# A two-block network in one kernel: its first norms, first products and the loads ahead of them, rearranged into one stage

## The chip, the cores and the metric

The kernel runs on one core of a Trainium2 chip. The metric is the device time of one execution in microseconds (us), here the median of several executions. TensorE is called PE in the profile, its weight loads PEld, VectorE DVE, ScalarE ACT, GpSimd POOL, and SyncE, which issues most loads, SP.

## The reference

A sequence of 1024 tokens of width 1024 passes through two blocks; a context of 256 tokens takes part in the first one. Only the beginning matters here:

```python
mod   = split(silu(c)     @ w_ada + b_ada, 6)      # sh1, sc1, g1, sh2, sc2, g2
mod_c = split(silu(c_ctx) @ w_ada + b_ada, 6)      # sh1c, sc1c, ...
h_lat = rmsnorm(x,   norm1_g) * (1 + sc1)  + sh1   # 1024 tokens
h_ctx = rmsnorm(ctx, norm1_g) * (1 + sc1c) + sh1c  # 256 tokens
u, v, q, k, vv, r, af, ab, ga, gb = split(h_lat @ w_in, ...)
# the same for h_ctx; then gated linear attention over both, a chunk MLP,
# a merge, a SwiGLU; then a second block (RG-LRU, window attention, SwiGLU)
```

`rmsnorm` divides by the root of the mean square over the 1024 channels and multiplies by the norm's weight. Everything is float32. A product with a weight matrix is computed from high and low parts: weights and activations are each split into a rounded high part and the rest, and three matmuls (high by high, low by high, high by low) are summed in PSUM.

## The kernel before, in words

Activations lie transposed, channels in the 128 partitions (8 tiles of 128 channels), tokens along the free dimension. The tokens are worked in three parts: the context (256 columns, tiles `CH`, `CL`) and two halves of x (512 columns each, tiles `XH`, `XL`). Weights come in tiles of 128 output channels, 128x1024 elements or 512 KB, in one fixed order (`weight_order`): first `al` (the low-rank gate inputs), then `k` 0 to 3, `vv` 0 to 7, `q`, and so on through the program. Each is loaded by SP into one of two raw slots `WS`, rounded by ACT into one of four slots `WH` (line 242) and subtracted by DVE into `WL` (line 250). `weights_sp`, `weights_act` and `weights_dve` bring this up to a given tile; they stand in the program order of the engine that runs them. Every engine executes its instructions in that order, and `wait_ge` stops it until a semaphore has its value.

`stage0` does the first norm. PE computes the modulation rows from `w_ada`, 8 tiles of 128x2048 elements (1 MB each, `ada_pe`, line 570): 8 by 4 products of 512 columns, each of two matmuls. ACT squares x and the context (lines 501, 505), DVE adds the squares over the 8 tiles (line 513), PE sums them over the partitions (`columns_pe`, line 578), ACT takes the root (line 606), DVE the reciprocal and a diagonal matrix of it, and PE spreads that over all partitions (`spread_pe`, line 564). ACT copies the modulation rows out of PSUM (line 618), PE turns them into columns (line 596), and DVE makes the four small vectors of scales and shifts (lines 644 to 648). Then `modulated_dve` and `modulated_act` make the modulated input of a part, per channel tile: DVE scales (line 538), ACT adds the shift and rounds (line 521), DVE takes the rest (line 531). `stage0` does so for the context and for the first half of x; SP's loads in it stand in the order of lines 481 to 492.

`stage1` begins with `firsts`, three groups of four products (`al`, `k0`, `k1`, `k2`), one group for each part of the tokens: 96 matmuls of 256 columns for the context, and twice 96 of 512 columns. `products_pe` (lines 273 to 296) runs a group with the channel tile k outermost, so each k needs only the tile k of the activations. The low-rank output goes to `AL` (lines 777 and 855), the three others through the four `TMP` slots to memory (lines 395 and 432). At the start of `stage1`, SP, ACT and DVE each wait for all that `stage0` has ended (`gone`):

```python
def sp_():
    for t in gone:
        SPW.wait_ge(*t)
    sp.dma_start(WA0[:], D["walpha"]).then_inc(*wal_in.up())
    sp.dma_start(cmask[:], D["cmask"]).then_inc(*cm_in.up())
    sp.dma_start(cb[:], D["crow"]).then_inc(*cb_in.up())
    weights_sp(NW + NS)
```

ACT then applies silu to `cb` and copies `WAL` ahead of its first copy out of PSUM, and the second half of x is modulated between the groups of the context and of the first half (`second_act`, `second_dve`). After `firsts`, `stage1` runs its fill, the products of `k3`, `vv` and `q`, beside the gates' decays; later stages follow in the same manner.

Of the kernel before, what the change touches and what calls it, by code (L numbers as in the profile page):

```python
# [7 lines left out]
F = mybir.dt.float32  # L8
R = mybir.dt.float32r
# [9 lines left out]
NW = 4  # L19
# [104 lines left out]
def program(nc, D, out):  # L124
# [69 lines left out]
    w_in = [sig("in", f"weight_in{s}") for s in range(NS)]  # L194
    w_hi, w_lo = sig("ac", "weight_high"), sig("dv", "weight_low")
# [37 lines left out]

    def weights_act(upto):
        while made["hi"] < min(upto, len(order)):
            i = made["hi"]
            made["hi"] += 1
            ACW.wait_ge(*w_in[i % NS].at(i // NS + 1))
            if i >= NW:
                ACW.wait_ge(*used[i - NW])  # L240
            n = cols_of[i]
            ac.activation(WH[:, i % NW, 0:n], WS[:, i % NS, 0:n], ACT.Copy).then_inc(*w_hi.up())  # L242

    def weights_dve(upto):
        while made["lo"] < min(upto, len(order)):
# [4 lines left out]
            dv.tensor_tensor(WL[:, i % NW, 0:n], WS[:, i % NS, 0:n], WH[:, i % NW, 0:n].bitcast(F), ALU.subtract).then_inc(*w_lo.up())  # L250

    def weights_sp(upto):
        while made["in"] < min(upto, len(order)):
            i = made["in"]
            made["in"] += 1
            if i >= NS:
                SPW.wait_ge(*w_lo.at(i - NS + 1))
            if i in raw_used:
                SPW.wait_ge(*raw_used[i])
            sp.dma_start(WS[:, i % NS, 0:cols_of[i]], tiles[i]).then_inc(*w_in[i % NS].up())  # L260
# [181 lines left out]
    def stage0():  # L442

        CH, CL = CTX
# [4 lines left out]
        DIA = {"c": RB[:, 512:768], 0: RB[:, 512:1024], 1: RB[:, 0:512]}  # L449
        cc_in, xc_in = sig("in", "cc"), sig("in", "xc")  # L450
        x_in = [sig("in", f"x{k}") for k in range(8)]
        ad_in = [sig("in", f"ad{k}") for k in range(8)]
        silu = sig("ac", "silu_c")
        ada = sig("pe", "ada")
        squares, added = sig("ac", "squares"), sig("dv", "squares_added")
        colsum, rooted, recip = sig("pe", "column_sums"), sig("ac", "rooted"), sig("dv", "reciprocal")
        diag, spread = sig("dv", "diagonal"), sig("pe", "spread")
        mcopy, mturn, mods = sig("ac", "mods_copied"), sig("pe", "mods_turned"), sig("dv", "mods")
        shifted = sig("dv", "shifted")
# [4 lines left out]

        sums = [("c", k) for k in range(8)] + [(h, k) for k in range(8) for h in range(2)]
        total = {"c": RB[:, 0:TC], 0: ACC[:, 0:512], 1: ACC[:, 512:1024]}
        first_of = {"c": 0, 0: 8, 1: 9}
        slots = [k for k in range(24) if sums[k][1] > 0]
# [3 lines left out]

        def source(what, k):
            s, c = dst[what][0], dst[what][1]
            return s[:, k, c:c + size[what]]

        def added_of(what):
            last = max(j for j in range(24) if sums[j][0] == what)
            return added.at(slots.index(last) + 1)

        def sp_():
            sp.dma_start(VEC[:], D["vec"]).then_inc(*vec_in.up())
            sp.dma_start(ident[:], D["ident"]).then_inc(*ident_in.up())
            sp.dma_start(sc2[:], D["cc"]).then_inc(*cc_in.up())
            loads = {2: (0, 1), 3: (2, 3), 4: (4, 5), 5: (6, 7)}
            for k in range(8):
                sp.dma_start(AD[:, k, :], D["ada"][k]).then_inc(*ad_in[k].up())
                if k == 2:
                    sp.dma_start(XC[:], D["ctxT"]).then_inc(*xc_in.up())
                for x in loads.get(k, ()):  # L490
                    sp.dma_start(RES[:, x, :], D["xT"][x]).then_inc(*x_in[x].up())
            weights_sp(NW)

        def squares_act(j):
            what, k = sums[j]
            if what == "c":
                ACW.wait_ge(*xc_in.at(1))
            else:
                ACW.wait_ge(*x_in[k].at(1))
            if k == 0:  # L500
# [22 lines left out]
        def modulated_dve(what):  # L523
# [11 lines left out]
            for k in range(8):  # L535
# [3 lines left out]
                if k:  # L539
                    low(k - 1)  # L540
# [3014 lines left out]
```

## Time and profile before

| | |
|---|---|
| median of 3 runs | 3434.43 us (3432.78 to 3436.52) |
| profiled execution | 3435.87 us |
| its span | 3434.6 us |
| PE busy | 3270.4 us (95%) |
| DVE, ACT, POOL busy | 1929.5, 1373.2, 384.1 us |
| mean granted PE clock | 0.98 |

The span runs from the first to the last recorded instruction; all positions below are us from its start. The granted clock is 1.00 where PE gets its full 2.4 GHz and 0.50 where it gets 1.2 GHz. A row of a timeline gives the start, the duration, engine, line, operation, the tiles written and read, the count of merged instructions, and in brackets how long the engine had been idle and what ended that.

### The profile page before, as it was taken

What the parts mean: (1) busy time and instruction counts of PE and PEld (TensorE: products, weight loads), DVE (VectorE), ACT (ScalarE), POOL (GpSimd) and SP (SyncE); (2) the same over time, 40 slices, a digit from 0 to 9 for tenths busy, and PEclk for the clock granted to TensorE, in tenths of its full rate; (3) what the DMA queues carried; (4) which work ended last, traced back from release to release, by engine and by line L of the source; (5) the groups of instructions that cost most, each with busy time, mean ns of one, the idle gap of its engine ahead of it and who ended that gap; (6) DMA issues with size and microseconds to landing.
All of it is one profiled execution on the core that took longest, in us unless ns stands there. A gap on an engine that the chain in (4) does not pass through costs nothing. (4 is left out here: it accounts for less than half of the span.)

```text
span 3434.6 us, 39599 instructions
## 1 busy us (share of the span) xinstructions
PE 3270.4 (95%) x14862; PEld 2659.9 (77%) x14862; DVE 1929.5 (56%) x3098; ACT 1373.2 (40%) x2320; POOL 384.1 (11%) x605
## 2 busy tenths in 40 slices
PE   6999999989999999999999999999788899999998
PEld 3888888877788878888888888877555678888886
DVE  4474343454334387777545555655576487777443
ACT  4592232224333244333233356554576343333221
POOL 0121000001100200000010101111211100001011
PEclk8999999999999999999999999999899899999999
DMA  5365433344553423333763433444844523334752
GB/s 218 107 218 183 142 126 123 123 156 157 200 161 117 138 71 117 109 115 118 248 203 97 154 119 137 136 157 150 171 96 104 184 92 117 105 116 165 248 179 77
DMA packets 228045, 494.14 MB, mean 144 GB/s; under 512 B 21520, under 2 KB 84624, under 8 KB 226320
## 3 DMA queue, kind: packets, MB, share of 16 engines
q1 hardware_dynamic: 147728, 302.30, 27.7%
q0 software_dynamic: 80128, 189.30, 16.9%
q8 instruction: 120, 1.97, 0.2%
q14 instruction: 69, 0.57, 0.0%
HBM read 353.63 MB, written 137.89 MB: 143 GB/s over the span
## 5 line engine op out<-in xcount | busy, mean ns | idle before, releaser
L290 PE MATMUL p<-s_xh,s_wh 128*128 128x512 f32 x2256 | 905.6, 401 | 36.9 <-DVE s_tmp L401 12.3
L291 PE MATMUL p<-s_xl,s_wh 128*128 128x512 f32 x2256 | 888.7, 394 | 0.0
L292 PE MATMUL p<-s_xh,s_wl 128*128 128x512 f32 x2256 | 888.2, 394 | 0.0
L290 PEld LDWEIGHTS p<-s_xh,s_wh 128*128 128x128 f32 x2256 | 430.9, 191 | 131.5 <-issue 20.2
L292 PEld LDWEIGHTS p<-s_xh,s_wl 128*128 128x128 f32 x2256 | 429.6, 190 | 92.3
L291 PEld LDWEIGHTS p<-s_xl,s_wh 128*128 128x128 f32 x2256 | 430.6, 191 | 89.6 <-issue 1.7
L2092 PE MATMUL p<-s_xh,s_wh 128*128 128x512 f32 x1152 | 449.5, 390 | 1.1 <-DVE s_xl L2199 1.0
L2094 PE MATMUL p<-s_xh,s_wl 128*128 128x512 f32 x1152 | 448.3, 389 | 0.0
L2093 PE MATMUL p<-s_xl,s_wh 128*128 128x512 f32 x1152 | 448.2, 389 | 0.0
L250 DVE TENSOR_TENSOR s_wl<-s_ws,s_wh 128x1024 fp32r<-128x1024 f32 x157 | 195.3, 1257 | 235.0 <-ACT s_wh L242 234.8
L2092 PEld LDWEIGHTS p<-s_xh,s_wh 128*128 128x128 f32 x1152 | 216.3, 188 | 47.7 <-issue 2.7
L2093 PEld LDWEIGHTS p<-s_xl,s_wh 128*128 128x128 f32 x1152 | 216.3, 188 | 45.1 <-issue 0.5
L2094 PEld LDWEIGHTS p<-s_xh,s_wl 128*128 128x128 f32 x1152 | 216.2, 188 | 44.9
L389 ACT ACTIVATE s_tmp<-p 128x512 f32<-128x512 f32 (+1 forms) x125 | 74.2, 594 | 432.8 <-PE p L292 432.7
L242 ACT ACTIVATE s_wh<-s_ws 128x1024 fp32r<-128x1024 f32 x157 | 162.7, 1049 | 76.3 <-PE p L292 33.7
L2232 ACT ACTIVATE s_wh<-s_ws 128x512 fp32r<-128x512 f32 x148 | 91.9, 625 | 146.7 <-PE p L2094 112.2
L2232 ACT ACTIVATE s_wh<-s_qb 128x512 fp32r<-128x512 f32 x140 | 87.2, 624 | 119.3 <-PE p L2094 109.8
L2443 POOL DMA_DIRECT2D d_h<-s_fhl x80 | 42.7, 533 | 756.0 <-DVE s_fhl L2338 723.4
L2333 DVE TENSOR_TENSOR s_wl<-s_ws,s_wh 128x512 fp32r<-128x512 f32 x148 | 106.3, 731 | 32.5 <-ACT s_wh L2232 32.3
L2333 DVE TENSOR_TENSOR s_wl<-s_qb,s_wh 128x512 fp32r<-128x512 f32 x140 | 100.1, 724 | 37.5 <-ACT s_wh L2232 37.3
L2238 ACT ACTIVATE s_fhl<-s_rb 128x512 fp32r<-128x512 f32 x80 | 50.7, 634 | 141.3 <-DVE s_rb L2376 135.0
L1459 POOL TENSOR_TENSOR s_acc<-s_acc,s_tmp 128x512 f32<-128x512 f32 x49 | 63.7, 1301 | 354.7 <-ACT s_tmp L1452 354.5
(380 smaller groups left out, 5099.8 us busy)
## 6 DMA issues: line engine op xcount, KB each, us to landing
d_h<-s_fhl POOLq DMA_DIRECT2D x80, 512.0 KB, 3.4
s_ws<-i_Wf SPq DMA_DIRECT2D x48, 512.0 KB, 4.3
s_qb<-i_Wf SPq DMA_DIRECT2D x40, 512.0 KB, 4.1
s_qb<-i_Wf SPq DMA_DIRECT2D x80, 256.0 KB, 3.1
s_ws<-i_Wf SPq DMA_DIRECT2D x80, 256.0 KB, 2.8
s_aw<-i_adaT SPq DMA_DIRECT2D x32, 512.0 KB, 3.7
s_xh<-d_h POOLq DMA_DIRECT2D x16, 1024.0 KB, 12.0
s_xl<-d_h POOLq DMA_DIRECT2D x16, 1024.0 KB, 15.7
```

What stands on the lines that cost most here:

```text
L242: ac.activation(WH[:, i % NW, 0:n], WS[:, i % NS, 0:n], ACT.Copy).then_inc(*w_hi.up())
L250: dv.tensor_tensor(WL[:, i % NW, 0:n], WS[:, i % NS, 0:n], WH[:, i % NW, 0:n].bitcast(F), ALU.subtract).then_inc(*w_lo.up())
L290: pe.matmul(o, wh, H[:, k, c:c + n], start=(k == 0), stop=False)
L291: pe.matmul(o, wh, L[:, k, c:c + n], start=False, stop=False)
L292: last = pe.matmul(o, wl, H[:, k, c:c + n], start=False, stop=(k == 7))
L389: ac.activation(o, ps, ACT.Copy, scale=p.scale).then_inc(*evA.up())
L1459: po.tensor_tensor(a, a, TMP[:, s.slot, :], ALU.add).then_inc(*sumP.up())
L2092: pe.matmul(o, wh[:, c], H[:, k, :], start=(start and k == 0), stop=False)
L2093: pe.matmul(o, wh[:, c], L[:, k, :], start=False, stop=False)
L2094: x = pe.matmul(o, wl[:, c], H[:, k, :], start=False, stop=(stop and k == 3))
L2232: ac.activation(half_tile(u.slot)[0], u.src, ACT.Copy).then_inc(*u_hi.up())
L2333: dv.tensor_tensor(l, u.src, h.bitcast(F), ALU.subtract).then_inc(*u_lo.up())
```

## The change

`stage0` and the first part of `stage1` (the three groups `firsts` with all that surrounds them) become one stage, and nothing waits for `gone` between them.

- Loads: `cc` and the first `w_ada` tile come first, then the context, `vec` and `ident`. The weight tiles 0 to 3 are loaded between `w_ada` tiles 2 to 5, tiles 2 and 3 into `ACC` and `RB` in place of `WS` (`raw_weights`). x comes as 16 pieces of 256 KB (a half of one channel tile each) in place of 8 of 512 KB, the first half's from behind `w_ada` tile 6 on. `cb`, `WA0` and `cmask` follow x without a wait.
- Squares go to memory of their own: those of the context to `TMP`, those of x over `w_ada` tiles that PE has used. Those of the second half are added by POOL.
- PE: the context's column sums and spread stand after `w_ada` tiles 2 and 4, the first half's column sums after tile 7, its spread inside the group of the context. The second half's column sums and spread stand inside the group of the first half.
- The modulation rows are copied by ACT and DVE, two each.
- ACT's and DVE's programs are rewritten as below; the context's keys leave PSUM through `ACC`, the second half's spread is copied to `RB`; silu of `cb` and the copy of `WAL` come near the end.
- The PSUM banks of the groups are others.

```diff
+    def raw_weights(i):
+        n = cols_of[i]
+        if 2 <= i < 4:
+            return (ACC, RB)[i - 2][:, 0:n], early_in[i - 2].at(1)
+        return WS[:, i % NS, 0:n], w_in[i % NS].at(i // NS + 1 if i < 2 else i // NS)
...
-            if i >= NS:
+            if i >= 4:
                 SPW.wait_ge(*w_lo.at(i - NS + 1))
...
+        SQ = {"c": [TF[:, 256 * k:256 * k + 256] for k in range(8)],
+              0: [adf[:, 1024 * k + 512:1024 * k + 1024] for k in range(8)],
+              1: [adf[:, 8192 + 1024 * k + 512:8192 + 1024 * k + 1024] for k in range(8)]}
...
+            if part == 1:
+                bank_free[6], bank_free[7], bank_free[4] = [rooted.at(2)], [], [shifted.at(8)]
+            if part == 2:
+                bank_free[5], bank_free[3] = [shifted.at(16)], [spread_copied.at(1)]
...
-                b = ((0, 1, 2, 3), (0, 4, 6, 7), (1, 2, 3, 5))[part][g]
+                b = ((0, 1, 2, 3), (6, 7, 4, 1), (0, 5, 2, 3))[part][g]
...
+        def sp_():
+            sp.dma_start(sc2[:], D["cc"]).then_inc(*cc_in.up())
+            for k in range(8):
+                sp.dma_start(AD[:, k, :], D["ada"][k]).then_inc(*ad_in[k].up())
+                if k == 0:
+                    sp.dma_start(XC[:], D["ctxT"]).then_inc(*xc_in.up())
+                    sp.dma_start(VEC[:], D["vec"]).then_inc(*vec_in.up())
+                    sp.dma_start(ident[:], D["ident"]).then_inc(*ident_in.up())
+                elif 2 <= k < 6:
+                    weights_sp(k - 1)
+                elif k == 6:
+                    x_sp(0, range(4))
+            x_sp(0, range(4, 8))
+            x_sp(1, range(8))
+            sp.dma_start(cb[:], D["crow"]).then_inc(*cb_in.up())
+            sp.dma_start(WA0[:], D["walpha"]).then_inc(*wal_in.up())
+            sp.dma_start(cmask[:], D["cmask"]).then_inc(*cm_in.up())
+            weights_sp(NW + NS)
...
+        def pe_():
+            for k in range(8):
+                ada_pe(k)
+                if k == 2:
+                    columns_pe("c")
+                if k == 4:
+                    spread_pe("c")
+            columns_pe(0)
+            PEW.wait_ge(*mcopy.at(2))
+            PEW.wait_ge(*mcopy_d.at(2))
+            for m in range(16):
+                last = pe.transpose(B[0][:, 2 * m:2 * m + 2], mrow[:, m * 128:m * 128 + 128], ident[0:2, 0:2])
...
+            products_pe(firsts[0], {3: lambda: spread_pe(0)})
+            products_pe(firsts[1], {1: lambda: columns_pe(1), 3: lambda: spread_pe(1)})
+            products_pe(firsts[2])
...
+        def act_():
...
+            for k in range(8):
+                square_act("c", k)
+            root_act("c")
+            weights_act(NW)
+            for k in range(8):
+                square_act(0, k)
+            ACW.wait_ge(*ada.at(8))
+            for c in range(2):
+                ac.activation(mrow[:, c * 512:c * 512 + 512], B[c][0:2, :], ACT.Copy).then_inc(*mcopy.up())
+            root_act(0)
+            for k in range(2):
+                square_act(1, k)
+            for k in range(8):
+                high_act("c", k)
+                if k < 6:
+                    square_act(1, 2 + k)
+            for k in range(2):
+                high_act(0, k)
+            ACW.wait_ge(*w_lo.at(3))
+            for g, p in enumerate(firsts[0][1:]):
+                ACW.wait_ge(*p.mm)
+                ac.activation(ACC[:, 256 * g:256 * g + 256], B[p.bank][:, 0:256], ACT.Copy).then_inc(*evA.up())
+            al_act(0)
+            root_act(1)
+            for k in range(2, 8):
+                high_act(0, k)
+            ACW.wait_ge(*spread.at(3))
+            ACW.wait_ge(*w_lo.at(4))
+            ac.activation(RB[:, 0:512], B[spread_bank[1]][:, :], ACT.Copy).then_inc(*spread_copied.up())
+            for k in range(8):
+                high_act(1, k)
+            al_act(1)
+            for p in firsts[1][1:]:
+                fill_act_first(p)
+            ACW.wait_ge(*wal_in.at(1))
+            ac.activation(WAL[:, :, :], WA0[:, :, :], ACT.Copy).then_inc(*wal_hi.up())
+            ACW.wait_ge(*cb_in.at(1))
+            ac.activation(cb[:, :], cb[:, :], ACT.Silu).then_inc(*cb_silu.up())
+            al_act(2)
+            for p in firsts[2][1:]:
+                fill_act_first(p)
...
+        def dve_():
...
+            for k in range(1, 8):
+                square_dve("c", k)
+            inverse_dve("c")
+            weights_dve(NW)
+            for k in range(1, 8):
+                square_dve(0, k)
+            DVW.wait_ge(*ada.at(8))
+            for c in range(2, 4):
+                dv.tensor_copy(mrow[:, c * 512:c * 512 + 512], B[c][0:2, :]).then_inc(*mcopy_d.up())
...
+            modulated_dve("c", {1: lambda: inverse_dve(0)})
+            modulated_dve(0, {5: lambda: inverse_dve(1)})
+            al_dve(0)
+            modulated_dve(1)
+            al_dve(1)
...
+            al_dve(2)
...
+        def pool_():
+            for k in range(1, 8):
+                POW.wait_ge(*squares.at(16 + k + 1))
+                POW.wait_ge(*added1.at(k - 1))
+                po.tensor_tensor(SQ[1][0], SQ[1][0], SQ[1][k], ALU.add).then_inc(*added1.up())
...
```

In `modulated_dve` the hook of step k runs after the low part of tile k - 1; in `products_pe` the hook of step k runs ahead of the matmuls of tile k.

## Rows read from the trace of the kernel before

**Rows 1.** Windows: length, then busy time (instructions) of each engine, PE clock, DMA share, GB/s.
```profile
10.00:20.00 10.00, 9.77 (x23) 1.84 (x22) 3.67 (x8) 4.75 (x12) 0.00 (x0) 1.00 1.01 419
...
50.00:60.00 10.00, 4.02 (x16) 3.52 (x16) 9.40 (x19) 4.58 (x10) 0.00 (x0) 0.50 0.00 0
...
70.00:80.00 10.00, 0.83 (x7) 0.62 (x6) 0.70 (x1) 4.09 (x7) 0.00 (x0) 0.79 0.64 236
```
**Rows 2.** Timeline of PE, 0 to 131 us.
```profile
7.46 12.19 PE L570 MATMUL p<-s_ad,s_sc 128*2 128x512 f32 x24 [7.46 <-DMA s_ad<-i_ada]
24.93 3.60 PE L570 MATMUL p<-s_ad,s_sc 128*2 128x512 f32 x8 [1.46 <-DMA s_ad<-i_ada]
...
29.98 3.60 PE L570 MATMUL p<-s_ad,s_sc 128*2 128x512 f32 x8 [0.92 <-DMA s_ad<-i_ada]
...
38.54 1.95 PE L578 MATMUL p<-s_ones,s_acc 128*128 128x1 f32 x16
...
43.94 1.98 PE L564 MATMUL p<-s_rb,s_ones 128*128 128x512 f32 x4
...
46.12 1.15 PE L596 MATMUL p<-s_ident,s_mrow 2*128 2x2 f32 x16 [0.19 <-ACT s_mrow L618]
...
50.88 0.55 PE L290 MATMUL p<-s_ch,s_wh 128*128 128x256 f32 x1 [3.62 <-DVE s_cl L531]
...
57.45 0.55 PE L290 MATMUL p<-s_ch,s_wh 128*128 128x256 f32 x1 [4.95 <-DVE s_wl L250]
...
62.13 0.30 PE L291 MATMUL p<-s_cl,s_wh 128*128 128x256 f32 x1
...
70.55 0.28 PE L292 MATMUL p<-s_ch,s_wl 128*128 128x256 f32 x1
81.11 0.76 PE L290 MATMUL p<-s_xh,s_wh 128*128 128x512 f32 x1 [10.28 <-DVE s_al L855]
...
86.24 0.40 PE L290 MATMUL p<-s_xh,s_wh 128*128 128x512 f32 x1
...
126.82 0.39 PE L292 MATMUL p<-s_xh,s_wl 128*128 128x512 f32 x1
130.19 0.36 PE L290 MATMUL p<-s_ch,s_wh 128*128 128x256 f32 x1 [2.98 <-DVE s_wl L250]
```
**Rows 3.** Timeline of DVE, 46 to 60 us.
```profile
47.86 0.87 DVE L538 SCALAR_TENSOR_TENSOR s_tmp<-s_xc,s_gs,p 128x256 f32<-128x256 f32 x2
50.29 0.48 DVE L531 SCALAR_TENSOR_TENSOR s_cl<-s_tmp,s_modc,s_ch 128x256 fp32r<-128x256 f32 x1 [1.56 <-ACT s_ch L521]
...
56.09 2.35 DVE L250 TENSOR_TENSOR s_wl<-s_ws,s_wh 128x1024 fp32r<-128x1024 f32 x2
58.35 1.40 DVE L538 SCALAR_TENSOR_TENSOR s_tmp<-s_res,s_gs,p 128x512 f32<-128x512 f32 x2
```
**Rows 4.** Timeline of ACT and SP, 44 to 76 us.
```profile
44.04 2.02 ACT L618 ACTIVATE s_mrow<-p 2x512 f32<-2x512 f32 x4 [1.37 <-PE p L570]
...
75.90 1.28 ACT L797 ACT_TABLE_LOAD   x1 [7.24 <-DMA s_cb<-i_crow]
...
70.39 0.43 SPq L742 DMA_DIRECT2D s_cb<-i_crow  x1
```
**Rows 5.** Groups by form, 0 to 48 us: count, busy us, mean ns, idle before.
```profile
L513 DVE TENSOR_TENSOR s_acc<-s_acc,s_tmp 128x512 f32<-128x512 f32 x14 | 9.7, 692 | 4.6 <-ACT s_tmp L505 3.5
L505 ACT ACTIVATE s_tmp<-s_res 128x512 f32<-128x512 f32 x14 | 8.0, 620 | 5.1 <-DMA s_res<-i_xT 4.7
```
**Rows 6.** Timeline, 3390 to 3397 us: one POOL addition and DVE beside it.
```profile
3396.27 1.29 POOL L1459 TENSOR_TENSOR s_acc<-s_acc,s_tmp 128x512 f32<-128x512 f32 x1 [6.87 <-ACT s_tmp L1452]
3396.74 2.10 DVE L2333 TENSOR_TENSOR s_wl<-s_ws,s_wh 128x512 fp32r<-128x512 f32 x2 [0.62 <-ACT s_wh L2232]
```
**Rows 7.** One line's view, L1459: duration of POOL's additions, ns min/median/max.
```profile
L1459 POOL TENSOR_TENSOR s_acc<-s_acc,s_tmp x49: 1260/1292/1804, 1136.3 to 3420.7; 128x512 f32<-128x512 f32 x49
```

**Rows 8.** The page's DMA issues: count, KB each, us from issue to landing.
```profile
s_ws<-i_Wf SPq DMA_DIRECT2D x80, 256.0 KB, 2.8
```

More of the change, by code:

```diff
@@ L471, in stage0 @@
         which = {"c": 0, 0: 1, 1: 2}
[L473 to L500, printed above, removed]
-                ac.activation(total[what], source(what, k), ACT.Square).then_inc(*squares.up())
-            else:
-                q = slots.index(j)
-                ACW.wait_ge(*added.at(q - NT + 1))
-                ac.activation(TMP[:, q % NT, 0:size[what]], source(what, k), ACT.Square).then_inc(*squares.up())
@@ L555, in stage0 @@
-        spread_bank = {"c": 7, 0: 4, 1: 5}
+        column_bank, spread_bank = {"c": 6, 0: 6, 1: 3}, {"c": 4, 0: 5, 1: 3}
         scale_of = {"c": GS[:, 8:16], 0: GS[:, 0:8], 1: GS[:, 0:8]}
         shift_of = {"c": MODC, 0: MOD, 1: MOD}
-        def spread_pe(what, free):
-            n = size[what]
-            PEW.wait_ge(*diag.at(which[what] + 1))
-            for t in free:
-                PEW.wait_ge(*t)
-            pe.matmul(B[spread_bank[what]][:, 0:n], ones[:], DIA[what], start=True, stop=True).then_inc(*spread.up())
@@ L566, in ada_pe @@
-        def ada_pe(k):
-            PEW.wait_ge(*silu.at(1))
-            PEW.wait_ge(*ad_in[k].at(1))
-            for c in range(4):
-                last = pe.matmul(B[c][0:2, :], sc2[:, k, :], AD[:, k, c * 512:c * 512 + 512], start=(k == 0), stop=(k == 7))
-            last.then_inc(*ada.up())
-        def columns_pe(what):
-            m = size[what] // 128
-            PEW.wait_ge(*added_of(what))
-            PEW.wait_ge(*const.at(1))
-            for j in range(m):
-                last = pe.matmul(B[4 + which[what]][:, j:j + 1], total[what][:, 128 * j:128 * j + 128], ones[:, 0:1], start=True, stop=True)
-            last.then_inc(*colsum.up())
@@ new lines, in ada_pe, with columns_pe @@
+        def ada_pe(k):
+            PEW.wait_ge(*silu.at(1))
+            PEW.wait_ge(*ad_in[k].at(1))
+            for c in range(4):
+                last = pe.matmul(B[c][0:2, :], sc2[:, k, :], AD[:, k, c * 512:c * 512 + 512], start=(k == 0), stop=(k == 7))
+            last.then_inc(*ada.up())
+        def columns_pe(what):
+            PEW.wait_ge(*{"c": added.at(7), 0: added.at(14), 1: added1.at(7)}[what])
+            PEW.wait_ge(*const.at(1))
+            if what == 1:
+                PEW.wait_ge(*spread3_free)
+            for j in range(size[what] // 128):
+                c = 4 * which[what] + j
+                last = pe.matmul(B[column_bank[what]][:, c:c + 1], SQ[what][0][:, 128 * j:128 * j + 128], ones[:, 0:1], start=True, stop=True)
+            last.then_inc(*colsum.up())
@@ L765, in pe_ @@
         def pe_():
-            for part, group in enumerate(firsts):
-                products_pe(group)
             for what, j in steps:
@@ L869, in pool_ @@
         def pool_():
-            for group in firsts:
-                for p in group[1:]:
-                    fill_pool(p)
             for what, j in steps:
```

362 lines of the change are left out of this document (159 added, 203 removed).

## The prediction, made before the changed kernel was run

> **What bounds the kernel now.** The page comes first: PE is busy for 95% of the span, so time is found only where PE waits, or runs at the low clock. The windows of the first 130 us are next, because the change touches nothing behind them. From 50 to 60 us PE is busy 4.02 of 10 us at a clock of 0.50, from 70 to 80 us 0.83 of 10 us [rows 1]. The timeline of PE then names the waits [rows 2]: 3.62 us before the first product (50.88) for the first low part of the context, 4.95 us at 57.45 for a weight's low part, 10.28 us at 81.11 for DVE's low part of `AL`. The timelines of the other engines say what stands behind these. At 47.86 DVE begins to modulate the context, and its first low part comes at 50.29 only, since ACT has two weight tiles to round first; the low parts of these tiles (56.09, 2.35 us) stand behind the whole context in DVE's order [rows 3]. The long wait is the border of the stages: SP issues the load of `cb` at 70.39, when everything of `stage0` has ended, and ACT waits 7.24 us for it (75.90), with the copy of `AL` behind [rows 4]. The groups of x then run without a gap from 81.11 to 126.82, then comes a wait of 2.98 us for the next weight [rows 2].
>
> So the end of the three groups, 126.82 + 0.23 = 127.05 us, is what the change can move. What follows is the same program behind the same weight wait (ACT and DVE reach tile 4 after the last group's copies in both), and I take it to shift as a whole.
>
> **The change part by part.** I work out when each step comes in the new order.
>
> *Loads.* The 24.93 and the 29.98 row wait for `w_ada` tiles with two x tiles between them, 2 MB in 5.05 us, or 2.53 us for a MB [rows 2]; the engines are full at 419 GB/s [rows 1]. By SP's order in the code 8.19 MB had been issued up to the tile of 24.93, so an arrival is 4.25 us plus 2.53 us for each MB ahead. In the new order the first tile is issued after one small load instead of three, at 0.43 us each (the cost of the `cb` issue [rows 4]), so the constant is 3.4 us. Tile 0 is there at about 6.3 us, tile 1 at 11.4 (the context is between), tile 4 at 21.6 (two weight tiles ahead), tile 7 at 12.19 x 2.53 + 3.4 = 34.2, the first half of x at 36.7, the second at 41.8.
>
> *PE up to the modulation.* The first tile takes 5.2 us (12.19 us for three, two at 3.42: 8 matmuls of 0.428 us), later ones 3.42 us [rows 2]. Tiles 0 to 2 end at 18.5; the context's sums (4 of the 16 in 1.95 us, about 0.6 with the change-over), tiles 3 and 4, its spread (0.6), tiles 5 and 6 end at 33.3; tile 7 comes at 34.2 and ends at 37.6. DVE's last addition of squares ends at 36.7 + 0.62 + 0.69 = 38.1 [rows 5] (a piece comes each 0.63 us, and both engines all but keep that pace). Column sums then take 1.0 (half of 1.95), the transposes 1.15 [rows 2], all four quarters of the rows being copied by then (half of ACT's 2.02 us from 37.7 [rows 4], DVE's two after its additions, about 39.6; DVE's copy isn't in the trace, 0.4 to 0.9 us each, I take 0.6). That gives 40.8, and 0.6 for the four small vectors (transposes' end 47.27 to 47.86) gives 41.4 against 47.86.
>
> *First product.* With the weights split long before (ACT's four roundings and DVE's four subtractions, 1.2 us each [rows 3], fit between 21 and 29 us, each tile landing in time), ACT is free: 0.48 for the scale, 0.5 for ACT, 0.59 from the low part's start to the product (50.29 to 50.88) [rows 2, 3]. First product at 43.0 instead of 50.88.
>
> *Group of the context.* At full clock a matmul of 256 columns takes (70.55 - 62.13) / 70 = 0.120 us, 96 take 11.5 us. ACT also has a square of x per k here, about 1.0 us per k in all, still under PE's 1.44. The spread of the first half adds 0.95 (half of 1.98 less overlap). The clock: before, it was at the 1.2 GHz level at 50.88, after 3.62 us without a matmul that followed small transposes, and needed the run from 57.45 to 62.13, 19 matmuls that at full clock take 2.28 us, to come back: 2.4 us lost. At 81.11 the same: 12 matmuls in 5.13 us that take 2.72 at full clock, 2.4 lost [rows 2]. Now PE pauses for 2.2 us (40.8 to 43.0) after small work since 37.6. The lower end is 0 (clock kept), the upper 4.8 (twice the row). I take 2.4, as the nearest row also had a short pause behind transposes. Sum: 43.0 + 11.5 + 0.95 + 2.4 = 57.9 for the end of the group.
>
> *Groups of x.* Between 86.24 and 126.82 lie 179 matmuls at 0.227 us [rows 2]; 192 take 43.5 us. Added inside are column sums (1.0) and spread (0.95) of the second half, that stood ahead of the first product before. Their waits: ACT cannot go on with the first half before it has emptied the context's banks and taken the second root. It does tiles 0 and 1, copies at 57.9, takes the root after the column sums at 57.9 + 2.7 + 1.0 = 61.6, and rounds tile 2 at 62.0; its low part is ready at about 63.5, when PE, having done tile 1, wants it at 64.3. Later tiles cost DVE 1.4 us (two of 0.70 [rows 3]) and PE 2.72. DVE's diagonal for the spread comes at about 67.3, PE reaches the place at 67.1: 0.2. The second half is modulated from 71.5 to 82.5, and PE wants its first tile at 83. So the end is 57.9 + 43.5 + 1.95 + 0.2 = 103.6.
>
> *Additions on POOL.* Seven at 1.29 us, at most 1.80 [rows 7], begin at 41.8 and end by 51, 54 at most; PE wants them at 60.6. But beside one POOL addition two DVE subtractions of 0.69 take 2.10, 0.7 more [rows 6]. At 0.7 for each addition the context's modulation becomes 5 us longer and ends at about 55 instead of 50. PE's last k begins at about 56, so this costs nothing with the clock at half, and up to 1 us if it is kept. I take 0.
>
> *Other edits.* Banks, the copy of the spread to `RB` (ACT, in the shade of PE's group), `ACC` for the context's keys, fewer `TMP` waits, and silu and `WAL` near the end each have a finished group or over 10 us of PE work as cover; bounds -0.5 and +1 us in all, taken as 0. Without that cover the table load for silu alone would cost 1.28 us [rows 4].
>
> *Sum.* 127.05 - 103.6 = 23.4 us less. The profiled execution becomes 3435.9 - 23.4 = 3412.5. It lay 1.4 us above the median of the runs, so the median becomes 3411.0. By parts: 10.3 for the wait at the border, 5.0 for the weight wait, 7.9 for the earlier first product, 2.4 for the second slow stretch, less 2.9 for sums and spreads moved between products and 0.2 of wait; and 0.9 for the group's first six matmuls, which took 1.6 us at the low clock (50.88 to 57.45 less the wait) where 0.7 is asked; their clock loss is now inside the 2.4.
>
> **The rivals.**
>
> *The clock is kept* into the first product: 2.4 us less, 3408.6. For it: the pause is 2.2 us, not 3.62, and the 1.46 us wait at 24.93 left the matmuls at full pace. Against it: almost nothing but transposes and column sums runs from 37.6 to 43.0.
>
> *Small loads are slow.* The trace has 256 KB loads that take 2.8 us from issue to landing [rows 8]. If the 16 pieces did not overlap, the first eight would need 22 us instead of 5, the modulation would begin 17 us later, and the time would be 3428. Against it: loads of 512 KB ran behind each other without any loss [rows 1], and I see no reason for a different rule at 256.
> The Trainium skill ("DMA: Bandwidth & Descriptors", "Measured (HBM→SBUF, 128 partitions, SWDGE, issued from GpSimd)") asks to batch DMAs to 1 MB or more for 75% of the peak. As an estimate by its fit (2.0 us and 436 GB/s) each piece would take 2.6 us; the trace's full engines with 512 KB loads in flight disagree with a serial reading.
>
> *A queue order stalls PE.* ACT stands at the context's banks, with six tiles of the first half behind. If a wait of the new order is later than I see (root, diagonal or a sum), PE waits inside the group of the first half, some 2 to 6 us: 3413 to 3417. For it: two of my margins are under 1 us. Against it: DVE and ACT need half of PE's time for a tile, so a late start is made up.
>
> *Slower: the clock stays low* through the context's and the first half's groups, since column sums and spreads break them. Then group one takes 20.5 us instead of 13.9 (96 at 0.213) and group two 41 instead of 21.8: 26 us, 3437. It decides if more than 45 us pass at 1.2 GHz. For it: from 50 to 57 us, with PE fed in pieces, the clock stayed at 0.50 [rows 1]. Against it: both recoveries came within 5.2 us of steady matmuls [rows 2], and the breaks are 1 us.
>
> **How the numbers follow.** Forecast 0.60, clock kept 0.17, queue stall 0.14, small loads 0.03, low clock 0.03, anything else 0.03. The own range of the likeliest is 3408 to 3414 (loads and squares 1 us each way, DVE's copies 0.5, spreads 1, the clock 1). The range is 3406 to 3417; it takes in the kept clock and most of the stall. About 0.2%, 7 us, is what a measurement of this kernel can tell from no change. All of the first three are faster, with most of the rest: 0.94 faster, 0.03 same, 0.03 slower.
>
> **What would show it.** The profile after should have the first product near 43, the group of 512 columns beginning near 58, no pause of PE over 1 us from there to 103 or 104, then again about 3 us for a weight, and the same length from there to the end. The `w_ada` tiles should be PE's bound (one wait under 1 us at the last). I am wrong in the large if the last matmul of the groups comes at 104 and the time is not 23 us less, that is, if the rest is not carried along whole; in the small if the first product is not at 43, or the groups are broken.

## The result, and the profile after

The changed kernel takes 3411.8 us (median of 4 runs, 3408.44 to 3415.9), the kernel before 3435.36 us beside it; the ratio is 0.9933, 95% interval 0.9916 to 0.995. It is 23.6 us faster; forecast were 23.4 us and 3411.0 us. The execution that was profiled took 3415.9 us (span 3414.6 us), the slowest of the four.

The page of the changed kernel shows in its first line what was won: PE has done the same work in a shorter span. POOL has 9.2 us more to do, the seven additions; the other engines stay within 3 us of before.

```profile
PE 3272.8 (96%) x14862; PEld 2661.8 (78%) x14862; DVE 1932.5 (57%) x3093; ACT 1373.6 (40%) x2319; POOL 393.3 (12%) x612
```

The timeline of PE in the changed kernel, 0 to 111 us, answers to [rows 2].

```profile
6.22 13.18 PE L563 MATMUL p<-s_ad,s_sc 128*2 128x512 f32 x24 [6.22 <-DMA s_ad<-i_ada]
...
27.46 10.64 PE L563 MATMUL p<-s_ad,s_sc 128*2 128x512 f32 x24
38.96 1.05 PE L573 MATMUL p<-s_ones,s_ad 128*128 128x1 f32 x8 [0.85 <-DVE s_ad L715]
40.19 1.12 PE L592 MATMUL p<-s_ident,s_mrow 2*128 2x2 f32 x16 [0.18 <-issue]
44.46 0.55 PE L299 MATMUL p<-s_ch,s_wh 128*128 128x256 f32 x1 [3.15 <-DVE s_cl L688]
...
47.84 0.55 PE L299 MATMUL p<-s_ch,s_wh 128*128 128x256 f32 x1 [0.48 <-DVE s_cl L688]
...
49.26 0.31 PE L299 MATMUL p<-s_ch,s_wh 128*128 128x256 f32 x1
...
59.46 0.40 PE L299 MATMUL p<-s_xh,s_wh 128*128 128x512 f32 x1
...
62.21 0.95 PE L573 MATMUL p<-s_ones,s_ad 128*128 128x1 f32 x8
...
68.61 1.02 PE L578 MATMUL p<-s_ad,s_ones 128*128 128x512 f32 x2
...
104.64 0.39 PE L301 MATMUL p<-s_xh,s_wl 128*128 128x512 f32 x1
108.12 0.55 PE L299 MATMUL p<-s_ch,s_wh 128*128 128x256 f32 x1 [3.08 <-DVE s_wl L258]
```

All of PE's waits in this stretch carry brackets. The wait of 4.95 us for a weight and the 10.28 us at the border are gone. From 59.46 the two groups of x run on to 104.64 with the column sums and the spread between their products and no wait. Their end is at 104.87 us (forecast 103.6), against 127.05. Left of the waits behind the modulation are 3.15 us ahead of the first product and 0.48 us inside the context's group; behind the groups stands the same wait for weight tile 4 (2.98 us before, 3.08 now).

POOL and then DVE between 41 and 48 us show why the first product is late; DVE's last row is the same line for the second half's diagonal, with POOL idle.

```profile
41.43 1.26 POOL L753 TENSOR_TENSOR s_ad<-s_ad 128x512 f32<-128x512 f32 x1 [40.98 <-ACT s_ad L603]
44.44 2.97 POOL L753 TENSOR_TENSOR s_ad<-s_ad 128x512 f32<-128x512 f32 x2 [1.75 <-ACT s_ad L603]
```

```profile
41.64 1.07 DVE L736 SCALAR_TENSOR_TENSOR s_gs<-s_mod,s_vec 128x8 f32<-128x8 f32 x1
42.63 0.15 DVE L737 SCALAR_TENSOR_TENSOR s_gs<-s_modc,s_vec 128x8 f32<-128x8 f32 x1
...
44.48 1.79 DVE L676 TENSOR_TENSOR s_ad<-s_ident,s_rc 128x512 f32<-128x512 f32 x1
46.20 0.47 DVE L698 SCALAR_TENSOR_TENSOR s_tmp<-s_xc,s_gs,p 128x256 f32<-128x256 f32 x1
46.59 1.11 DVE L688 SCALAR_TENSOR_TENSOR s_cl<-s_tmp,s_modc,s_ch 128x256 fp32r<-128x256 f32 x1
...
67.62 0.69 DVE L676 TENSOR_TENSOR s_ad<-s_ident,s_rc 128x512 f32<-128x512 f32 x1
```

The instruction at 41.64 has 8 elements per partition. The same kind took 0.15 us a moment later, but this one 1.07 us: it ends at 42.71, just when POOL's addition (41.43 + 1.26 = 42.69) has ended. The diagonal at 44.48 took 1.79 us, where its like took 0.69 at 67.62. The scaling at 46.20, one of whose two tensors is in PSUM, kept its 0.47 us. A low part took 1.11 us, against 0.48 us in [rows 3]. That POOL is the reason, and not ACT or the loads beside it, is only shown by the run with the additions on DVE below.

### The profile page after: what moved, and what is told of

Same layout as the page of the kernel before. It is cut to its first block and busy times, and to the rows that moved or that the text cites. A ratio compares the mean times of both kernels' runs of the same rounds, so it can differ in the third digit from the quotient of the medians.

```text
span 3414.6 us, 39602 instructions
## 1 busy us (share of the span) xinstructions
PE 3272.8 (96%) x14862; PEld 2661.8 (78%) x14862; DVE 1932.5 (57%) x3093; ACT 1373.6 (40%) x2319; POOL 393.3 (12%) x612
## 5 line engine op out<-in xcount | busy, mean ns | idle before, releaser
L2264 ACT ACTIVATE s_fhl<-s_rb 128x512 fp32r<-128x512 f32 x80 | 50.7, 634 | 141.3 <-DVE s_rb L2402 135.1
```

## The experiments

The positions below are from the profiled execution of each kernel. "Start of `k3`" is the first matmul behind the three groups: 130.19 us before, 108.12 us in the changed kernel.

### The border alone, in the kernel before

```diff
             weights_sp(NW)
+            sp.dma_start(WA0[:], D["walpha"]).then_inc(*wal_in.up())
+            sp.dma_start(cmask[:], D["cmask"]).then_inc(*cm_in.up())
+            sp.dma_start(cb[:], D["crow"]).then_inc(*cb_in.up())
```

This is in `sp_()` of `stage0`; the same three loads are removed from `stage1`, where they stood behind the wait for `gone`, and their tiles get memory that both stages keep.

> One part of the change alone, put into the kernel before: the loads of `WA0`, `cmask` and `cb` are issued by SP at the end of `stage0`, behind the first four weight tiles, and wait for nothing; their tiles have memory of their own. Everything else, ACT's order with silu and the copy of `WAL` ahead of the context's copies included, stays. Theory (the border wait is the load's 7.2 us of waiting plus ACT's and DVE's work in a row): ACT starts silu at 69.4, when DVE has ended the first half, instead of at 75.9; the copy of `AL` follows at about 72.8 and PE's first matmul of 512 columns comes at 74.7 instead of 81.11. The groups end at 120.6 instead of 127.05, 6.4 us less, and the time falls by as much. So about 4 of the 10.3 us at the border belong to ACT's and DVE's order and not to the load. Rival (the load is the whole wait): PE's wait all but disappears, 71 to 72 for the first matmul of 512 columns, and 10 us less. Rival (something else frees the bank late): the matmul stays at 80 or later and nothing is gained.

Measured: 3428.27 us, 0.9981 of the time before (0.9967 to 0.9996). The timeline of PE, then of ACT and DVE:

```profile
75.38 0.77 PE L290 MATMUL p<-s_xh,s_wh 128*128 128x512 f32 x1 [4.59 <-DVE s_al L850]
...
123.54 0.55 PE L290 MATMUL p<-s_ch,s_wh 128*128 128x256 f32 x1 [2.98 <-DVE s_wl L250]
```

```profile
70.17 1.28 ACT L792 ACT_TABLE_LOAD   x1 [0.94 <-DVE s_xl L534]
```

```profile
73.56 1.22 DVE L843 TENSOR_TENSOR s_wal<-s_wa,s_wal 32x1024 fp32r<-32x1024 f32 x1 [3.55 <-ACT s_wal L794]
74.81 0.42 DVE L850 TENSOR_TENSOR s_al<-p,s_al 32x256 fp32r<-32x256 f32 x1
```

`k3` starts 6.65 us earlier (expected 6.4). The border's wait fell from 10.28 to 4.59 us, so more than half of it was the load behind `gone`; the 4.6 us that stay are, by these rows, ACT's table load, silu and copy of `WAL` (from 70.17) and DVE's two low parts in a row (to 75.23). The first product of x itself came 5.73 us earlier, later than the expected 74.7; the other 0.9 us are the low clock behind it, which ended 3.1 us after this product (at 78.46) where it took 5.1 us before [rows 2]. So the fit of 6.65 to 6.4 is in part luck. The load as the whole wait is refuted, a late bank by something else too.

### Silu and `WAL` ahead of the context's copies

```diff
 # act_()
             ACW.wait_ge(*w_lo.at(3))
+            ACW.wait_ge(*firsts[0][3].mm)
+            ACW.wait_ge(*wal_in.at(1))
+            ac.activation(WAL[:, :, :], WA0[:, :, :], ACT.Copy).then_inc(*wal_hi.up())
+            ACW.wait_ge(*cb_in.at(1))
+            ac.activation(cb[:, :], cb[:, :], ACT.Silu).then_inc(*cb_silu.up())
             for g, p in enumerate(firsts[0][1:]):
...
```

The same waits and activations are removed from ahead of `al_act(2)`.

> The changed kernel with one part undone in ACT's order: the copy of `WAL` and silu of `cb`, with its table load, stand ahead of the context's copies, right behind the last product of the context's group, as they did before. The loads stay early. Theory (the place of these instructions is worth PE time even when their data is there): ACT needs 3.4 us (1.04, 1.28, 1.06) before its first copy, and another 1.28 for the root's table again. PE waits 1.6 us for a free bank at channel tile 0 of the first half's group, about 0.4 at tile 2 and 1.1 for the diagonal, and the groups end about 3.2 us later, near 108. Rival (PE's group of 21.8 us hides it, as DVE and ACT need half of PE's time per tile): no wait over 0.3 us, end unchanged at 104.9. Rival (the wait is passed on in full): 4.7 us later.

Measured: 3418.87 us, 0.9954 (0.9932 to 0.9977). PE, then ACT:

```profile
63.71 0.50 PE L299 MATMUL p<-s_xh,s_wh 128*128 128x512 f32 x1 [1.77 <-ACT s_acc L651]
...
110.55 0.36 PE L299 MATMUL p<-s_ch,s_wh 128*128 128x256 f32 x1 [3.08 <-DVE s_wl L258]
```

```profile
59.96 1.06 ACT L646 ACTIVATE s_wal<-s_wa 128x1024 fp32r<-128x1024 f32 x1 [2.40 <-PE p L301]
61.04 1.28 ACT L648 ACT_TABLE_LOAD   x1
62.33 1.06 ACT L648 ACTIVATE s_cb<-s_cb 128x1024 f32<-128x1024 f32 x1
...
64.50 1.28 ACT L609 ACT_TABLE_LOAD   x1
```

`k3` starts 2.4 us later (expected 3.2). The bank's wait of 1.77 us is there, as is the second table load at 64.50. The smaller waits I expected, at tile 2 and at the diagonal, do not show as waits for data. The first product of x came 0.25 us later than in the changed kernel's profile already (59.71 against 59.46), which is no effect of the edit, and the product behind the wait 2.18 us later (63.71 against 61.53). So the place of three ACT instructions, with all their data there, is worth about 2 us here. The medians differ by 7 us from that of the changed kernel, but the two intervals overlap. That the same three cost more at the border of before (the 4.6 us above, with DVE's two low parts) is read from the rows and was not run by itself.

### The second half's additions on DVE

```diff
+        def second_sums():
+            for k in range(1, 8):
+                DVW.wait_ge(*squares.at(16 + k + 1))
+                DVW.wait_ge(*added.now())
+                dv.tensor_tensor(SQ[1][0], SQ[1][0], SQ[1][k], ALU.add).then_inc(*added.up())
...
-            modulated_dve(0, {5: lambda: inverse_dve(1)})
+            modulated_dve(0, {2: second_sums, 5: lambda: inverse_dve(1)})
...
-            for k in range(1, 8):
-                POW.wait_ge(*squares.at(16 + k + 1))
-                POW.wait_ge(*added1.at(k - 1))
-                po.tensor_tensor(SQ[1][0], SQ[1][0], SQ[1][k], ALU.add).then_inc(*added1.up())
```

> The changed kernel, with the seven additions of the second half's squares on DVE instead of POOL. They stand behind the low part of channel tile 1 of the first half, where DVE sat idle for 4.56 us in the trace of the changed kernel. Theory (POOL's additions slow DVE's two-source instructions beside them): the vector instruction at 41.64 that took 1.07 us takes 0.17, the diagonal of the first half takes 0.69 instead of 1.79, the low parts of the context take 0.48 instead of 1.1 to 1.35, the first product starts at 43.5 instead of 44.46, the wait of 0.48 us inside the group of the context goes, and the additions (4.9 us) end before PE asks for the column sums near 61. The groups end about 1.5 us earlier, near 103.4. Rival (the long durations come from ACT's squares or from the loads, not from POOL): the durations stay, the first product stays at 44.5, and the end moves by less than 0.3. Rival (the additions on DVE come too late): PE waits for the column sums by 1 us or more and the end does not move or is later.

Measured: 3409.75 us, 0.9923 (0.9894 to 0.9952). DVE, then PE:

```profile
42.14 0.17 DVE L742 SCALAR_TENSOR_TENSOR s_gs<-s_mod,s_vec 128x8 f32<-128x8 f32 x1
...
44.09 0.69 DVE L676 TENSOR_TENSOR s_ad<-s_ident,s_rc 128x512 f32<-128x512 f32 x1
...
45.09 0.48 DVE L688 SCALAR_TENSOR_TENSOR s_cl<-s_tmp,s_modc,s_ch 128x256 fp32r<-128x256 f32 x1
```

```profile
44.07 0.55 PE L299 MATMUL p<-s_ch,s_wh 128*128 128x256 f32 x1 [2.25 <-DVE s_cl L688]
...
106.45 0.36 PE L299 MATMUL p<-s_ch,s_wh 128*128 128x256 f32 x1 [3.08 <-DVE s_wl L258]
```

All three durations are back at what they are without company, the pause ahead of the first product is 2.25 instead of 3.15 us, there is no wait inside the context's group, and `k3` starts 1.67 us earlier (expected 1.5). So POOL's additions held DVE up. The 1.67 us are not all theirs. The two waits give 0.9 and 0.48 us; the loads came 0.5 us later in this execution (its transposes began at 40.70 and not at 40.19), and the low clock ended earlier, at about 47 us and not at 49.3, which gives back another 0.8. With the medians' spread of some us the whole time alone could not have shown it.

### Extra matmuls in PE's pause

```diff
             last.then_inc(*mturn.up())
+            for _ in range(3):
+                pe.matmul(B[7][:, :], ones[:], XC[:, 0:2, :].rearrange("p a b -> p (a b)"), start=True, stop=True)
             products_pe(firsts[0], {3: lambda: spread_pe(0)})
```

> The changed kernel, with three extra matmuls of 512 columns (all-ones matrix by the context's raw input, into PSUM bank 7, whose content nobody uses) between the transposes and the first product, in the 3.15 us pause. Nothing is left out. Theory (PE's clock falls since between the last modulation product at 38.1 and the first product at 44.46 it has next to no matmul work): the extra matmuls take 2.6 us, all inside the pause; the granted clock stays at 1.00 from 41 to 50, the group of the context takes about 2.1 us less (the time from 44.46 to 49.3 at the low clock for 20 matmuls that need 2.4 at the high one), and the groups end near 102.7. Rival (the clock would fall all the same, by what PE does over a longer stretch): it is 0.50 in the group and the end moves by less than 0.3 us. Rival (the extra work is in the way): the first product comes later than 44.6.

Measured: 3411.98 us, 0.9922 (0.9899 to 0.9944). Two windows (clock, DMA share and GB/s are the last three), then the timeline of PE:

```profile
37.00:41.00 4.00, 2.96 (x18) 1.52 (x17) 3.26 (x5) 2.79 (x6) 0.00 (x0) 1.00 1.06 388
41.00:44.00 3.00, 3.00 (x16) 1.95 (x16) 1.85 (x6) 1.00 (x3) 1.26 (x1) 0.54 1.05 402
```

```profile
40.65 1.39 PE L592 MATMUL p<-s_ident,s_mrow 2*128 2x2 f32 x16 [0.18 <-issue]
41.98 5.49 PE L595 MATMUL p<-s_xc,s_ones 128*128 128x512 f32 x6
46.48 1.20 PE L299 MATMUL p<-s_ch,s_wh 128*128 128x256 f32 x1
```

The clock was at 0.50 before the extra work had begun: the mean of 0.54 from 41 to 44 us puts the fall near 41.2, and the first extra matmul is at 41.98. Six matmuls took 5.49 us instead of 2.6, and the first product came at 46.48 instead of 44.46; the clock then rose sooner, at about 48, and `k3` started at 108.64, with loads that were 0.5 us later than in the changed kernel's profile. The theory fell: the clock was down before the pause behind the transposes could begin. What lies ahead of it in this execution is a wait of 0.86 us for the column sums and then only column sums and transposes (from 39.42 on); the next run fills that wait too.

### One extra product earlier

```diff
+        def spare_pe(n):
+            for _ in range(n):
+                pe.matmul(B[7][:, :], ones[:], XC[:, 0:2, :].rearrange("p a b -> p (a b)"), start=True, stop=True)
...
+            spare_pe(1)
             columns_pe(0)
...
             last.then_inc(*mturn.up())
+            spare_pe(2)
```

> The changed kernel with extra work on PE: one product of 512 columns (two matmuls, result unused, PSUM bank 7) right behind the last modulation product, in the 0.86 us that PE waits for the column sums there, and two behind the transposes. The run with three behind the transposes alone had its clock at 0.50 before the first of them ended, since it falls about 1 us after the transposes, and the extra matmuls then took 0.85 us each. Theory (the light work from 38.1 on, not the pause behind the transposes, is what the clock answers to, and one product there is enough to hold it): the granted clock is 1.00 from 38 to 50, the first product stays at 44.5, the group of the context ends near 57.4 instead of 59.46. Rival (it takes more work, the column sums and transposes weigh nothing): the clock falls near 42 or 43 as before, the four extra matmuls at the end take 3.4 us, and the first product is at 45.0.

Measured: 3413.85 us, 0.9945 (0.9922 to 0.9967). The timeline of PE:

```profile
38.51 1.12 PE L582 MATMUL p<-s_xc,s_ones 128*128 128x512 f32 x2
...
41.73 3.53 PE L582 MATMUL p<-s_xc,s_ones 128*128 128x512 f32 x4
44.95 0.55 PE L299 MATMUL p<-s_ch,s_wh 128*128 128x256 f32 x1
...
48.32 0.36 PE L299 MATMUL p<-s_ch,s_wh 128*128 128x256 f32 x1 [1.46 <-DVE s_cl L694]
```

The clock was 0.51 from 42 to 44 us all the same; the four matmuls took 3.53 us, the first product came at 44.95, and `k3` started at 108.23. The rival holds: one more product is not enough. Neither pause is then what the clock answered to here; that it was the light work is what is left, and no run takes that work away. The clock was back at about 45.4 us, 3.8 us sooner than in the changed kernel's profile, and yet nothing was won: PE now ran ahead of DVE, whose low parts still lay beside POOL's additions, and waited 1.46 us for one at 48.32. So filling the pause gains nothing in the two forms tried, but the second was held back by the other fault; the two edits together, this filling and the additions on DVE, were not run. What would keep the clock through these 6 us stays open.

### x in whole tiles

```diff
-        x_in = {(h, k): sig("in", f"x{h}{k}") for h in range(2) for k in range(8)}
+        x_in = {(0, k): sig("in", f"x{k}") for k in range(8)}
+        x_in.update({(1, k): x_in[(0, k)] for k in range(8)})
...
             for k in ks:
-                sp.dma_start(RES[:, k, 512 * h:512 * h + 512], D["xT"][k][:, 512 * h:512 * h + 512]).then_inc(*x_in[(h, k)].up())
+                if h == 0:
+                    sp.dma_start(RES[:, k, :], D["xT"][k]).then_inc(*x_in[(0, k)].up())
```

> The changed kernel with x loaded as 8 whole channel tiles of 512 KB instead of 16 halves of 256 KB, in the same places of SP's order: tiles 0 to 3 between the `w_ada` tiles 6 and 7, tiles 4 to 7 behind. 2 MB more stand ahead of the first half's last piece. Theory (loads keep one pace of 2.53 us for a MB whatever their size, and the first half's squares wait for them): the first half is complete 5.1 us later, the column sums start at 44.1 instead of 38.96, the first product at 49.6 instead of 44.46, and the first product of `k3` at 113.2 instead of 108.12. Rival (pieces of 256 KB are slow, so whole tiles make up for their number): 2 us or less. Rival (PE's modulation products are the bound and not the loads): the column sums move by the delay of `w_ada` tile 7 alone, 1 us or so.

Measured: 3417.89 us, 0.9954 (0.9935 to 0.9974). The timeline of PE:

```profile
37.26 3.60 PE L565 MATMUL p<-s_ad,s_sc 128*2 128x512 f32 x8 [2.56 <-DMA s_ad<-i_ada]
...
43.76 1.05 PE L575 MATMUL p<-s_ones,s_ad 128*128 128x1 f32 x8 [2.91 <-DVE s_ad L717]
...
49.27 0.55 PE L299 MATMUL p<-s_ch,s_wh 128*128 128x256 f32 x1 [3.10 <-DVE s_cl L690]
...
112.53 0.36 PE L299 MATMUL p<-s_ch,s_wh 128*128 128x256 f32 x1 [3.08 <-DVE s_wl L258]
```

The column sums moved by 4.8 us, the first product by 4.81, `k3` by 4.41 (expected 5.1 for each). The last `w_ada` tile, with 1 MB more ahead of it, came at 37.26 instead of 34.64 to 35.01. What counts is how many bytes stand ahead of a piece; how large it is counts little. The halves do cost something: from 38 to 42 us, while x is loaded in both, the DMA engines moved 391 GB/s in the changed kernel and 410 with whole tiles, 5% more. The Trainium skill's advice to batch DMAs to 1 MB ("DMA: Bandwidth & Descriptors", "Measured (HBM→SBUF, 128 partitions, SWDGE, issued from GpSimd)") would have spoken for larger pieces and so for the slower version here, where loads queue behind one another.

### The next weight ahead of the last copies

```diff
             al_act(2)
+            weights_act(NW + 1)
             for p in firsts[2][1:]:
                 fill_act_first(p)
```

> The changed kernel with one instruction moved: ACT rounds weight tile 4 (`k3`) right behind the last copy of `AL`, ahead of the three copies of the last group, instead of behind them. Theory (the 3.08 us wait for tile 4's low part is ACT's three copies, its rounding and DVE's subtraction in a row): the rounding starts at 103.6 instead of 105.56, the subtraction at 104.65, and PE waits 1.0 us instead of 3.08; `k3` starts at 106.0 instead of 108.12. If the clock is then kept, 1.5 to 3 us more come back behind it. Rival (the next thing is late: the copies of the last group, now 1 us later, or the load of the following tile): the wait moves to the second or third product of the fill and the rest is not earlier.

Measured: 3411.63 us, 0.9934 (0.9912 to 0.9957). The timeline of PE:

```profile
105.34 0.39 PE L301 MATMUL p<-s_xh,s_wl 128*128 128x512 f32 x1
106.78 0.36 PE L299 MATMUL p<-s_ch,s_wh 128*128 128x256 f32 x1 [1.05 <-DVE s_wl L258]
```

The wait fell from 3.08 to 1.05 us, as expected, with no new one in the next products; `k3` started at 106.78 (expected 106.0). The groups ended 0.7 us later than in the changed kernel's profile, since the clock was at 0.50 from about 40.5 to 50.7 us in this execution, and the whole time shows no gain. Alone it is inconclusive in the time.

### Both improvements, and the changed kernel again

The last run takes the additions on DVE and the weight ahead of the copies together; the changed kernel ran again beside it, five executions of each.

> The changed kernel again, unaltered, for its own spread and as the reference of the next one on the same chip. Expected: 3411.8 us as before, 0.9933 of the time of the kernel before; `k3` starts at 108 within 0.6 us; the granted clock at the wait for tile 4 falls in some executions and is kept in others, and spans differ by 2 to 3 us from this alone.

> The changed kernel with the second half's additions on DVE (as tried alone: 1.67 us less at the start of `k3`) and weight tile 4 rounded ahead of the last three copies. Theory (the two savings lie in different waits and add): `k3` starts at 104.4 instead of 108.12, 3.7 us less, and the median is 3 to 5 us below the changed kernel's, near 3407.5; 0.992 of the kernel before. Rival (the fill behind is bound by ACT, which is busy 49 of 50 us from 150 to 200, and gives the earlier start back): `k3` starts early but the end comes less than 1.5 us earlier.

Measured: the changed kernel 3414.7 us (3408.36 to 3416.79), 0.9932 of before (0.9919 to 0.9944); with both improvements 3408.18 us (3406.06 to 3414.31), 0.9919 (0.9906 to 0.9933). `k3` started at 107.90 and 105.06 us. The timeline of PE, first of the changed kernel:

```profile
107.90 0.36 PE L299 MATMUL p<-s_ch,s_wh 128*128 128x256 f32 x1 [3.08 <-DVE s_wl L258]
```

And of the one with both:

```profile
44.24 0.55 PE L299 MATMUL p<-s_ch,s_wh 128*128 128x256 f32 x1 [2.25 <-DVE s_cl L689]
...
105.06 0.36 PE L299 MATMUL p<-s_ch,s_wh 128*128 128x256 f32 x1 [1.05 <-DVE s_wl L258]
```

The profiled executions differ by 3.7 us in span (3410.6 and 3406.9) and by 2.8 us at `k3`, where I had expected 3.7 us against 108.12. Of the 2.8 us the weight's wait gives 2.03, as expected; the additions on DVE gave 0.8 and not the 1.67 I had added, half of which was the clock of that one execution. The medians differ by 6.5 us, but the two intervals overlap. The version is faster than before beyond doubt; that it beats the changed kernel rests on the trace's two shorter waits more than on the times. The giving back by the fill was not seen in this pair of profiles.

## Why the prediction was right

The mechanism held, and the time is within 1 us, though the interval of the ratio alone leaves room for 17 to 29 us. By its own steps:

- **Loads.** An arrival by 3.4 us plus 2.53 us a MB gave 6.3 us for the first `w_ada` tile (6.22) and 34.2 for the last. Six executions with this order of loads show PE's wait for it ending between 34.64 and 35.01, 0.4 to 0.8 us late; in the one shown above no wait for it shows. That the size of the pieces does not matter was argued from loads of 512 KB; the run with whole tiles shows it true to 5% of the rate.
- **PE up to the modulation.** The last modulation product was put at 37.6 and ended about 38.1. DVE's last addition of squares was put at 38.1 and ended at 38.91, its two copies at 39.6 and ended at 40.09, the transposes at 40.8 and ended at 41.31. The step that was short is DVE's chain of additions behind the last piece: 0.8 us, of which 0.5 reached the transposes.
- **The four small vectors.** 0.6 us were forecast, and it took 1.5 us, from the transposes' end at 41.31 to 42.82. This is the mis-sized term. I had seen from [rows 6] that POOL's additions slow DVE and priced it on the long low parts only, where PE's pace hides it. The first addition falls on the tiny instruction that stands right on the path: 0.9 us. The run with the additions on DVE gives it back. By my own times the two would not have met (vectors done at 41.4, first addition at 41.8), but the vectors came 0.5 us later and the addition 0.4 us earlier. The price was misread too. I took 0.7 us for each addition; the loss is what is left of the addition when the DVE instruction starts. The trace of before has this as well, where this subtraction, begun 0.48 us into POOL's addition (3388.11 to 3389.40), ended 0.55 us behind it:

```profile
3388.59 1.36 DVE L2333 TENSOR_TENSOR s_wl<-s_qb,s_wh 128x512 fp32r<-128x512 f32 x1 [0.62 <-ACT s_wh L2232]
```

- **First product.** 43.0 forecast, 44.46 measured: 0.5 from the sums, 0.9 from POOL.
- **The context's group.** 14.9 us forecast, 15.0 measured (44.46 to 59.46). The low clock ended at 49.26; 18 matmuls had taken 4.8 us where 2.2 are due (my later expectation counts 20). Of the 2.6 us too many 0.5 are the wait and 2.2 the clock, near the 2.4 that I took. That size is in part luck: the low clock reached 2.9 us into the group in the run with the additions on DVE, 3.4 us in the second profile of the changed kernel and 6.1 us in the run with the weight first. Of the two reasons I gave for the fall, the pause and the small work ahead of it, the pause is not needed, as the extra matmuls showed.
- **The groups of x.** 45.65 us forecast (43.5, 1.95 and 0.2), 45.41 measured, with no wait. The root, the diagonal and the sums came in time; the column sums follow directly on tile 0. The margins under 1 us held: DVE's diagonal ended at 68.31 and PE took it at 68.61. What three ACT instructions more in front cost, about 2 us, was a wait for a bank at tile 0 and none of those that the prediction had named (root, diagonal, a sum).
- **The rest carried whole.** It was: `k3` starts 22.1 us earlier, and 22.1 is also 23.4 less the 1.3 us of the steps above. What comes on top is the scatter of executions. In the profiled one the lead at the end was 20.0 us, in the second profile of the same kernel 24.0 us. At the wait for tile 4 the first has the low clock behind it and the second does not, in their windows (clock, DMA share and GB/s are the last three):

```profile
108.00:110.00 2.00, 1.88 (x9) 1.92 (x10) 1.10 (x1) 0.00 (x0) 0.00 (x0) 0.50 0.56 131
```

```profile
108.00:110.00 2.00, 2.00 (x17) 2.00 (x18) 0.89 (x1) 0.00 (x0) 0.00 (x0) 1.00 0.54 125
```

But this is not what parts them at the end. A later landmark is the first of POOL's 49 additions to `acc`, at 1136.3 us before [rows 7]. The first profile, then the second:

```profile
L1485 POOL TENSOR_TENSOR s_acc<-s_acc,s_tmp x49: 1261/1295/1811, 1113.5 to 3400.8; 128x512 f32<-128x512 f32 x49
```

```profile
L1485 POOL TENSOR_TENSOR s_acc<-s_acc,s_tmp x49: 1256/1293/1798, 1112.9 to 3396.0; 128x512 f32<-128x512 f32 x49
```

There the leads are 22.8 and 23.4 us. The two are 0.6 us apart, and most of their 4.0 us arises behind, in stages that the change does not touch. The rest was carried whole as far as this scatter of some 2 us each way lets one see.

So the median's fit to 1 us is partly luck: the trace's own measure, the end of the groups, was off by 1.3 us of 23.4.

Of the parts of the sum, the border (5.7 us of the load) and the order of the loads have runs of their own; the earlier first product (7.9 us) and the weight's wait (5.0 us) are read from the two traces and were not taken apart.

Of the rivals, the kept clock did not come, small loads were refuted, no queue stalled PE in the groups, and the clock rose in the context's group.

## What to carry to other kernels

An engine's program order at a border between stages is a wait that can be split: here 5.7 us of 10.3 were a load held back by a wait for everything, and the rest, by the rows, instructions standing ahead of a bank's release. Loads that queue behind each other arrive by the bytes ahead of them, so the piece that the next step needs should come first, even in halves of 256 KB at 5% less rate. Before work is moved to POOL, look at every DVE instruction with two inputs in SBUF on the critical path beside it, the shortest too: what it can lose is the rest of POOL's instruction, not a share of its own length. And before a gain is added to another, ask how much of it was the clock of one execution.

## What the runs showed of the hardware

- A DVE instruction that reads two tensors from SBUF, started while POOL adds two tensors, ended only after POOL's instruction: 1.07 us for one of 0.17 us (ending at 42.71, POOL's at 42.69), and 1.79 us for one of 0.69 us. In the run with the weight first the same small instruction began later, at 42.43, took 0.43 us and ended at 42.86, POOL's addition at 42.83. One with a tensor in PSUM kept its 0.47 us. The diagonal fits a full block too: begun at 44.48, it ended at 46.27, which is one addition of 1.26 us from 44.44 and then 0.57 us. By the Trainium skill ("SBUF — State Buffer", "Who interferes with whom") a DVE instruction with two SBUF inputs contends with a GpSimd instruction that reads SBUF, and of two that want the shared ports the later one waits out the other's whole instruction. The trace agrees, with 0.9 us lost on an instruction of 8 elements.
- In the eight executions with the changed kernel's order of loads the granted clock fell to 0.50 between about 40.4 and 43.6 us, near the column sums and transposes (38.96 to 41.31 in the first profile, where it fell at about 42.4), though PE was busy by the profile for most of the time up to their end. A product of 512 columns ahead of the column sums did not change it. Matmuls in the gap behind then run at the low clock themselves: 5.49 us for six.
- The same wait of 3.08 us at weight tile 4 was followed by the low clock in some executions of one kernel and not in others.
- Loads in one queue moved 391 GB/s in pieces of 256 KB and 410 GB/s in pieces of 512 KB (38 to 42 us, the changed kernel and the run with whole tiles).
